# A two-block decoder kernel in float32: lead of the weight splits counted in split pieces, modulation pieces spread, second block by halves of tokens

## What is computed

```python
for l in range(2):                                   # first block
    x = x + token_mixers(rmsnorm(x, mix_norm_g[l]))  # retention, SSD, GLA, mLSTM; gates; w_branch; w_out
    h = rmsnorm(x, ffn_norm_g[l])
    x = x + (swiglu(h) if l == 0 else moe_ffn(h))    # 8 experts, top 2, width 2816
x = rmsnorm(x, final_norm_g)
for l in range(2):                                   # second block
    shift_m, scale_m, gate_m, shift_f, scale_f, gate_f = split(silu(c) @ ada_w[l] + ada_b[l], 6)
    h = rms_norm(x, g_pre_mix[l]) * (1 + scale_m) + shift_m
    q, k, v, u = split(h @ w_in[l] + b_in[l])        # 512, 128, 128, 512 columns
    mix = concat(windowed_attention(rope(q), rope(k), v, sinks), pooling(u)) @ w_out[l]
    x = x + gate_m * rms_norm(mix, g_post_mix[l])
    h = rms_norm(x, g_pre_ffn[l]) * (1 + scale_f) + shift_f
    x = x + gate_f * rms_norm((silu(h @ w_gate[l]) * (h @ w_up[l])) @ w_down[l], g_post_ffn[l])
```

## Time and profile before

| | us |
|---|---|
| median of three runs | 2360.64 |
| profiled execution, its own time | 2357.28 |
| span of the profiled execution | 2355.5 |
| TensorE (PE) busy | 2131.1 |
| VectorE (DVE) busy | 1555.6 |
| ScalarE (ACT) busy | 1185.7 |

### The profile page before, as it was taken

The page is one execution under the profiler, slowest core; times in us unless marked ns, Lnnn a source line. Parts: engine busy times, 40 slices in busy tenths (PEclk is TensorE's granted clock), DMA queues, the critical chain, the costliest instruction groups (busy, mean ns, idle before and its releaser), DMA issues.

```text
span 2355.5 us, 25505 instructions
## 1 busy us (share of the span) xinstructions
PE 2131.1 (90%) x10570; PEld 1738.3 (74%) x10570; DVE 1555.6 (66%) x1533; ACT 1185.7 (50%) x1259; POOL 62.2 (3%) x87
## 2 busy tenths in 40 slices
PE   5899789997999877999999999999967899778997
PEld 5687557886777656888888888888756688666886
DVE  3666465554567554899989989999855544555443
ACT  4444234443444233777777777777623444334433
POOL 0000001000000001000000000000000100101000
PEclk9999989998999988999999999999978899888999
DMA  7455665553556572999999999999952465423551
GB/s 255 161 199 201 230 227 182 183 192 108 169 206 215 196 280 88 341 361 363 360 350 364 367 344 361 367 366 365 365 173 72 145 212 190 163 71 126 190 185 53
DMA packets 369318, 550.47 MB, mean 234 GB/s; under 512 B 21030, under 2 KB 295078, under 8 KB 362150
## 3 DMA queue, kind: packets, MB, share of 16 engines
q1 hardware_dynamic: 365168, 534.82, 66.7%
q10 hardware_dynamic: 4028, 13.95, 1.6%
HBM read 547.58 MB, written 1.15 MB: 233 GB/s over the span
## 4 chain that ended last, share of the span: by engine, by line
PE 82%; DVE 9%; ACT 5%; DMA 2%; POOL 1%; issue 1%; ACTq 0%; DVEq 0%; POOLq 0%
PE bank L418 78%; DVE wlo L919 3%; PE bank L446 2%; ACT whi L913 1%; PE bank L505 1%; POOL small L1946 1%; DMA raw<-in_w_branch 1%; DVE arena L1367 1%; ACT xn L982 0%; DMA xn<-in_lmask 0%; DMA small<-in_sinks 0%; DVE xn L1425 0%; DVE gate_tanh L1421 0%; ACT rowbuf L1001 0%; POOL small L1944 0%
## 5 line engine op out<-in xcount | busy, mean ns | idle before, releaser
L919 DVE TENSOR_TENSOR wlo<-raw,whi 128x2048 fp32r<-128x2048 f32 x461 | 1051.0, 2287 | 343.2 <-ACT whi L913 343.0
L913 ACT ACTIVATE whi<-raw 128x2048 fp32r<-128x2048 f32 x461 | 878.3, 1909 | 289.2 <-PE bank L418 254.8
L418 PE MATMUL bank<-whi,hThi 128*128 128x512 f32 (+2 forms) x1104 | 440.8, 399 | 40.9 <-DVE wlo L919 28.5
L418 PE MATMUL bank<-wlo,hThi 128*128 128x512 f32 (+2 forms) x1104 | 431.9, 391 | 0.0
L418 PE MATMUL bank<-whi,hTlo 128*128 128x512 f32 (+2 forms) x1104 | 431.7, 391 | 0.0
L418 PEld LDWEIGHTS bank<-whi,hThi 128*128 128x128 f32 x1104 | 213.9, 194 | 101.0 <-DVE wlo L919 35.4
L418 PE MATMUL bank<-whi,slots_hi 128*128 128x512 f32 x704 | 280.4, 398 | 1.9 <-DVE slots_lo L1720 1.9
L418 PE MATMUL bank<-wlo,slots_hi 128*128 128x512 f32 x704 | 275.3, 391 | 0.0
L418 PE MATMUL bank<-whi,slots_lo 128*128 128x512 f32 x704 | 275.1, 391 | 0.0
L418 PEld LDWEIGHTS bank<-whi,hTlo 128*128 128x128 f32 x1104 | 212.6, 193 | 44.0
L418 PEld LDWEIGHTS bank<-wlo,hThi 128*128 128x128 f32 x1104 | 213.6, 194 | 40.5
(11 more groups left out here) (286 smaller groups left out, 2378.6 us busy)
## 6 DMA issues: line engine op xcount, KB each, us to landing
raw<-in_moe_w SPq DMA_DIRECT2D x352, 512.0 KB, 6.1
raw<-in_moe_w SPq DMA_DIRECT2D x88, 1024.0 KB, 7.6
raw<-in_w_in SPq DMA_DIRECT2D x72, 1024.0 KB, 5.7
raw<-in_ada_w SPq DMA_DIRECT2D x48, 1024.0 KB, 5.7
raw<-in_ffn_w SPq DMA_DIRECT2D x44, 512.0 KB, 4.8
raw<-in_w_gate SPq DMA_DIRECT2D x44, 512.0 KB, 4.0
raw<-in_w_up SPq DMA_DIRECT2D x44, 512.0 KB, 5.0
raw<-in_w_down SPq DMA_DIRECT2D x22, 1024.0 KB, 5.0
```

What stands on the lines that cost most here:

```text
L418: m = mm(dst, l_, r_, start=start and i == 0, stop=stop and i == len(pairs) - 1)
L913: s.then_inc(s.unit.activation(split_slot(whi, p)[:, 0:n], slot_of_ring(raw, p, NRAW)[:, 0:n], ACT.Copy), ("hi", p), sem="weights_hi")
L919: e.then_inc(e.unit.tensor_tensor(split_slot(wlo, p)[:, 0:n], slot_of_ring(raw, p, NRAW)[:, 0:n], split_slot(whi, p)[:, 0:n].bitcast(F32), ...
```

## The change

In words:

- `look_ahead` sets the lead in split pieces only: up to AHEAD (2) split pieces behind the current one, at most 3 beyond the oldest unread, and within 5 plan places of it. It is set at each `piece()` and again when a piece is read. `split_ahead` lets ScalarE and VectorE split a named piece at a given place of their own program; `t.ahead` lowers the lead to 1 or 0 at some places.
- `MIXER_T`: the d steps stand one at a time through the whole mixer; the gates g3 between the gla levels are cut into quarters of 12 matmuls (one token tile each).
- Feed-forward: transposes of chunk i-1 now before `down` of i-2; the last two `down` run token tile by token tile; the first `up` runs tile by tile, each behind its own features.
- First block's ends: adding, squares, scale and features go tile by tile. The last scatter uses the "middle" banks.
- `joined`: the final norm of the first block and the first modulated norm of the second share one chain; both roots from sums of x and of x times gain.
- Second block: v and k first, then q by halves, scores between the u products, all transposes and the pooling in pairs, the pooled half of `w_out` before the attended half. `norm_and_add` works tile by tile, multiplies gate and scale before the roots are known, and one fused instruction after each.
- Start: x in two DMAs, tables in parts, masks as uint8 from the host; the first weight pieces wait for nothing. The result leaves in two DMAs. Loads of modulation and attention tables move earlier on ScalarE's queue.

The diff, cut to its core:

```diff
+    def split_ahead(self, name, n):
+        at = [p for p, z in enumerate(self.board.plan) if z[0] == name]
+        self.reach = max([self.reach] + [p + 1 for p in at[:n]])
+        self.split()
...
+    def look_ahead(self):
+        pieces, first = self.board.split_pieces, (self.unread or [self.taken])[0]
+        here, oldest = bisect_left(pieces, self.taken), bisect_left(pieces, first)
+        behind = pieces[here:min(here + self.ahead, oldest + NSPLIT)]
+        self.reach = max([self.reach] + [p + 1 for p in behind if p < first + NRAW])
...
             if name[0] == "read" and name[1] in self.unread:
                 self.unread.remove(name[1])
+                self.look_ahead()
...
-                    "gla0", "d10", "g3.0a", "gla1", "d11", "d12", "gla2", "g3.0b", "gla3", "d13", "d14", "gla4", "g3.1a", "gla5", "d15", "d16",
+                    "g2.0a", "ml3", "d15", "g2.0b", "d16", "g2.1a", "ml6", "d17", "g2.1b", "d18", "gla0", "d19", "gla1", "g3.0a0", "gla2", "g3.0a1", "gla3",
...
-                t.reach = max(t.reach, min(t.taken + AHEAD, (t.unread or [p])[0] + NSPLIT))
+                t.look_ahead()
...
+                    if 1 <= i <= len(todo):
+                        turn(i - 1)
                     if i >= 2:
...
+                        if nt == 1 or i < len(todo):
+                            read, parts = down_weights(i - 2)
+                            down(i - 2, parts, ys, read)
+                        elif i == len(todo) + 1:
+                            both = [down_weights(i - 3), down_weights(i - 2)]
+                            for tt in range(nt):
+                                for n in range(2):
+                                    down(i - 3 + n, both[n][1], ys[2 * tt:2 * tt + 2], both[n][0])
...
+                head_scores(0, 0)
+                head_scores(1, 0)
+                rotate(1)
+                both = []
+                for tt in range(NT):
+                    for half in range(2):
+                        if tt == 0:
+                            both.append(piece(("u2", l), half_piece(w, 4 * half, 768)))
+                        t.ahead = 0 if tt else AHEAD
+                        token_product(("u2", l), both[half][1], here, half, tt, "all", *([both[half][0]] if tt else []))
...
+            def norm_and_add(where, gate, names, then=None, stage=None):
...
+                v.wait_ge(("gate_in", *gate))
+                gated(0, 0)
+                gated(0, 1)
+                add(0)
+                if then:
+                    scale(0)
+                gated(1, 0)
+                if then:
+                    shift(0)
+                gated(1, 1)
+                if then:
+                    features(stage, None, (0,))
+                add(1)
+                if then:
+                    scale(1)
+                    shift(1)
+                    features(stage, None, (1,))
...
+                        v.split_ahead(("wout2", l, 1), 1)
...
+            for tt in range(NT):
+                d.then_inc(d.unit.dma_start(x3[:, tt], a["x"][0, pick_tokens(tt), :]), ("x_in", tt), sem=f"x{tt}_in", by=16)
-            d.wait_ge("constants")
             for p, (_, _, _, loads) in enumerate(plan):
...
+                if p == 2:
+                    d.then_inc(d.unit.dma_start(cst[:, FIRST:], a["const"][:, FIRST:]), sem="tables_in", by=16)
```

More of the change, by code:

```diff
@@ L58, with bisect_left @@
 AHEAD = 2
+def bisect_left(sorted_list, value):
+    return sum(z < value for z in sorted_list)
 class Idle:
@@ L334, in program @@
         inner.close()
+        attention.close()
         stage.close()
@@ L447, in transposes, with features @@
                 return m
-            def features(src3, stage, ready, tokens=range(NT)):
+            def features(src3, stage, ready, tokens=range(NT), ring="all"):
                 for tt in tokens:
@@ L802, in second_mixer, with values, queries @@
-                rotate(0)
+                def values(tt):
+                    for half in range(2):
+                        t.wait_ge(("hT", here, tt, 4 * half))
+                        m = product(v_bank[:, tt * P:(tt + 1) * P], [(stat_tokens(k, tt), (wf[0][:, k, P:2 * P], wf[1][:, k, P:2 * P]))
+                                                                     for k in range(4 * half, 4 * half + 4)], half == 0, half == 1)
+                    return m
+                def queries(i):
+                    read, parts = piece(("q2", l, i), full_piece(w, i * 2 * P))
+                    for j in range(2):
+                        bank = t.take(("q2", l, i, j))
+                        m = project_features(full(parts), j * P, here, bank, 0)
+                        t.then_inc(m, ("full", ("q2", l, i, j)), *([read] if j else []))
+                        yield
@@ L807, in second_mixer @@
-                bank = t.take(("v2", l))
-                for tt in range(NT):
-                    m = product(bank[:, tt * P:(tt + 1) * P], [(stat_tokens(k, tt), (wf[0][:, k, P:2 * P], wf[1][:, k, P:2 * P]))
-                                                               for k in range(KD)])
-                t.then_inc(m, ("full", ("v2", l)), read)
-                rotate(1)
+                t.then_inc(project_features(wf, 0, here, bank, 0), ("full", ("k2", l)), read)
+                first, second = queries(0), queries(1)
@@ L813, in second_mixer @@
+                next(first)
                 bank = t.take(("swap", l))
@@ new lines, in weigh_values @@
+                def weigh_values(tt, ring):
+                    bank = t.take(("att_out", l, tt), ring)
+                    t.wait_ge(("probT", l, tt), ("v", l))
+                    for h in range(QH):
+                        kv = slice((h // 4) * HD, (h // 4 + 1) * HD)
+                        m = group(bank[:, h * HD:(h + 1) * HD],
+                                  [(probT_[tt][:, h, kt * P:(kt + 1) * P], vt3[:, kt, kv]) for kt in range(tt + 1)])
+                    t.then_inc(m, ("full", ("att_out", l, tt)))
@@ new lines, in turn_outputs, with mix_out @@
+                def turn_outputs(tt, ring):
+                    bank = t.take(("attT", l, tt), ring)
+                    t.wait_ge(("attended", l, tt))
+                    t.then_inc(transposes(bank, [attended[tt][:, c * P:(c + 1) * P] for c in range(4)]), ("full", ("attT", l, tt)))
+                def mix_out(hf, half, tt, parts, *done):
+                    name, wq = (("wout2", l, hf), tt), quarter(parts)
+                    bank = t.take(name, "low") if half else t.bank(name)
+                    m = product(bank[:, :], [(stat_tokens(4 * half + k, tt), (wq[0][:, k], wq[1][:, k])) for k in range(4)],
+                                start=half == 1, stop=half == 0)
+                    t.then_inc(m, *([] if half else [("full", name)]), *done)
@@ L940, in way @@
                 else:
-                    e.wait_ge("way_end")
+                    e.reach = max(e.reach, board.need.get((part, "way_end"), 0))
+                    e.split()
                 e.own()
@@ L982, in square, with features @@
                 s.then_inc(act(dst3[:, tt, :], src3[:, tt, :], ACT.Square, accum_out=stat[:, at + tt:at + tt + 1]), name)
-            def features(stage, scale=None):
-                for tt in range(NT):
+            def features(stage, scale=None, tokens=range(NT)):
+                for tt in tokens:
                     for k in range(0, KD, 4):
@@ L2072, in constant_tables @@
     add("ident", np.eye(P))
+    add("power", np.full((P, 1), -0.5))
     half = HD // 2
```

743 lines of the change are left out of this document (418 added, 325 removed), and 5 rows, old and new, of the table MIXER_T.

## The result

The changed kernel took 2203.83 us (median of four runs, 2203.47 to 2204.67), the kernel before 2360.76 beside it. The ratio is 0.9338, with a 95% interval of 0.9322 to 0.9354. The forecast was 2203.

The account below looks back on a forecast made before the run. TensorE was taken to bound the kernel, with 224.4 us idle and 71 us lost to low clock. Idle terms of 123 us plus 34 of clock, 157 in all, gave 2203 us, range 2180 to 2235.

Parts of the forecast that it names:

- What can be won: Whole kernel: 224 us of TensorE idle and 71 us of slow matmuls; nothing in the full expert stage.
- Start, 11: Kernel start: first weight piece no longer waits for the tables, 11 us less idle (8 to 13).
- The lead, 38: Mostly the two token mixers: earlier splits remove three quarters of 51.5 us of `wlo` waits, 38 us (15 to 50).
- 5 of the row: Modulation row: single d steps remove TensorE's two waits for ScalarE's copy of the last chunk, 5 us (3 to 5).
- 4.5 of the merge: Merge in the two mixers: one split less in each chain, 4.5 us of 6.5 (2 to 6.5).
- Feed-forwards, 8: Feed-forwards: transposes go ahead of `down`, removing 8 us of the 9.0 of `gatedTlo_ffn` waits (5 to 9).
- First block's norms, 7.5: First block: tile 0's chain runs during tile 1's last matmuls, 7.5 us of 12.3 (3 to 8.5).
- Second block's norms, 26: Norm waits before and in the second block: tile 0 first, 26 us of 46.0 (12 to 34).
- Attention, 20: Attention: pooling copies on VectorE, scores between u products, 20 us of 27.2 of waits (10 to 25).
- End, 3: Kernel end: shorter two-root chain and half the result leaving earlier, 3 us of 10.0 (1 to 5).
- Clock, 34: TensorE's low-clock stretches: half of their 71 us price, less a little, comes back, 34 us (12 to 58).
- the first rival: Mixers: splits only change places with other waits; lead 15 instead of 38, clock 20 instead of 34; 2240 us, chance 0.18.

Follow-up runs that it names:

- the kernel with transposes as fill: Changed kernel plus unread transposes of the identity where TensorE would wait, ahead of the router and four second-block stages: 2199.83 us, ratio 0.9333.

## Why the prediction was right

The time was right to a microsecond, which the parts were not; that they cancelled so closely is luck. By the prediction's own steps:

- **What can be won.** Right. The experts' 755 us did not move, and the gain came out of idle time (127.6 against 123) and clock (26.0 against 34).
- **Start, 11.** 10.0 measured from first product to first product, with the first weight piece issued at 1.64.
- **The lead, 38, with 5 of the row and 4.5 of the merge.** Too small: these are 47.5 of idle, while undoing lead and table together gives back 154.3 - 96.8 = 57.5 us of idle and 18 of busy time. All of the `wlo` waits went, 51.5 behind the start, which is the high end that I had set. The discount of a quarter was for splits that pass other work; I had named the price, but put it on the lead alone. The runs show that it belongs to the lead with the old table (26.8 us of `scoresB`; with the new one the new waits at the scans are 8.6), and that the new table, which I had given only 5 us for the row, is what pays it off: 26 us by the ratios.
- **Feed-forwards, 8.** 8.8 of idle; 8.5 us of time by the ratios.
- **First block's norms, 7.5.** Too large. Without the start, the waits for the norm fell from 12.3 to 5.3, all of it the router's (3.8 before, though I had left it 4), but those for `hTlo` at these places rose by 3.7 (6.2 to 14.4 - 4.5). About 3 are left.
- **Second block's norms, 26.** `xn` fell from 46.0 to 21.2, by 24.8; waits for the features (L1352 before, L1496 now) rose from 1.5 to 8.1. So 18 net. Of the 14.3 before the second block I had taken 7 away; 10.0 are left, not 7.3.
- **Attention, 20.** 27.2 of waits became 2.4 for `qrot` and 1.4 for the attended features, 23 less; the high end was 25. A wait of 2.1 for the sinks' load went as well, which no term had. No experiment undid this part by itself, so its share of the clock stays open.
- **End, 3.** 10.0 - 6.4 = 3.6.
- **Clock, 34.** 26.0. I took nearly half of the 71 for half of the idle time gone. The low stretches ahead of and between the second block's layers stayed and grew, from 20.48 to 27.30 us and from 17.07 to 20.48, with 16.43 and 17.12 us of busy time in them instead of 6.97 and 7.21. TensorE runs transposes and 128-column products between short waits there. Whether that kind of work is why they last is argued, not shown.

The too small terms of the mixers and of attention and the too large ones of clock and norms cancelled. The idle parts found, 10.0, 57.5, 8.8, 3, 18, 23, 2.1 and 3.6, add up to 126 of the 127.6 us. Of the whole gain, the mixers' lead and table are 73 us by the ratios, where the prediction had 47.5 and, as its share of the clock, 13. For the rest, undoing the transposes gave 8.5, VectorE's order by tiles 13 and the wait at the start 12. What remains, some 50 us, attention above all, is attributed by the waits alone.

Of the marks set beforehand, first product near 14, no wait for `rowbuf`, fewer than 20 low stretches, idle near 100, the experts at 755, modulated norm near 20 and attention under 7 came true. Those of 20 us of `wlo` and of 75 us in low stretches did not (0 and 86.4). One sign of being wrong was set too loosely: steps of VectorE's scans did appear as new releasers in the mixers (`scoresB` 4.2, `arena` 2.0), and yet the first rival did not hold.

The first rival (splits only change places with other waits) had the right mechanism for a kernel that was not run as the change: it is what the new lead does on the old table. The Trainium skill's rule in "TensorE: Matmul & The Clock Gate", Part 1, puts the ramp under 1% of a typical kernel's span. It stands there for the warm-up at a kernel's start, and it does not carry over to a clock that falls again many times: by half of the busy time in the low stretches behind the start the price was 3.0% before and is 2.0% now (86.4 / 2 = 43.2 of 2201.9).

## What to carry to other kernels

A lead for work done ahead on an engine that takes its steps in order has two limits: what the consumer needs, and what has landed. Counting only the items that need the work served the first here (no `wlo` waits). It ran into the second where the other items in the same ring were bunched (26.8 us of `scoresB`), and hardly where they were spread (4.2). Before such a rule is judged, look at what stands in the queue behind the item done ahead, and undo the two parts of the change both singly and together, since here 64 and 26 made 73.

## What the runs showed of the hardware

A stretch of low clock can last while TensorE is nearly always busy: 16.03 of 17.07 us in the kernel with transposes as fill, in a stretch of transposes and 128-column products. Work put in the waits changed the time by nothing that can be told if it was transposes, though the clock rose within a run of 50 of them (at 1621.13) and 75.5 us of busy time, fill included, were left at the lower level instead of 86.4. With 512-column float32 matmuls 61.3 us were left, and the time gained was 5 to 7 us, with overlapping intervals.

Behind the expert code, where its two ways (sparse and dense) join, the engines start late. In the kernel's code each of them waits there until TensorE, ScalarE and VectorE have ended their way, which the profile shows as "issue". In the changed kernel ScalarE begins its squares at 1614.18. In the kernel of transposes, TensorE's first fill, which reads only constants, comes 5.0 us behind the scatter, and 3.6 us behind VectorE's last sum (1612.77):

```profile
1610.80 2.06 DVE L1872 SCALAR_TENSOR_TENSOR x<-bank,small,x 128x512 f32<-128x512 f32 x3
...
1614.18 1.06 ACT L1346 ACTIVATE pooled<-x 128x1024 f32<-128x1024 f32 x1 [5.59 <-issue]
...
1616.13 1.23 DVE L1954 TENSOR_TENSOR xn<-x,final_gain 128x1024 f32<-128x1024 f32 x1 [3.27 <-issue]
```

VectorE's last sum ends at 1612.9. Up to there ScalarE waits for the join, though it needs only the first token tile; 1.3 us more pass until its first square. So the 10.04 us wait before the second block holds both, the join and a late start behind it. What in the join takes the time was not tried.
